# Where the turn of the heavy activations and the border's piece stand in an expert step

## The reference, cut to what matters

```python
for i in range(DEPTH):                       # DEPTH = 2, SEQ = 256, D_MODEL = 1024
    ...                                      # attention and recurrent branches
    xn2 = rmsnorm(h, ffn_norm[i])
    if i % 2 == 0:
        h = h + swiglu(xn2, dense_w1[j], dense_w3[j], dense_w2[j])
    else:
        h = h + moe_ffn(xn2, router_w[j], router_b[j], moe_w1[j], moe_w3[j], moe_w2[j])
    ...                                      # per-layer embedding

def moe_ffn(xn, router_w, router_b, w1, w3, w2):
    ...                                      # gate: top 2 of 8 experts, softmax over the two
    for e in range(N_EXPERTS):
        out = out + gate[..., e:e + 1] * swiglu(xn, w1[e], w3[e], w2[e])   # D_FF = 3584
```

## Time and profile before

| | us |
|---|---|
| median of 3 runs (1691.14 to 1693.38) | 1693.28 |
| the profiled execution, its own time | 1692.69 |
| its span, first to last instruction | 1690.8 |
| PE busy | 1671.0 |
| ACT busy, DVE busy | 877.3, 1072.1 |

### The profile page before, as it was taken

The page is one execution under the profiler, slowest core; times in us unless marked ns, Lnnn a source line. Parts: engine busy times, 40 slices in busy tenths (PEclk is TensorE's granted clock), DMA queues, the critical chain, the costliest instruction groups (busy, mean ns, idle before and its releaser), DMA issues.

```text
span 1690.8 us, 25482 instructions
## 1 busy us (share of the span) xinstructions
PE 1671.0 (99%) x10246; PEld 1299.1 (77%) x10246; DVE 1072.1 (63%) x1662; ACT 877.3 (52%) x1349; POOL 19.2 (1%) x51
## 2 busy tenths in 40 slices
PE   9999999999999999998999999999999999999998
PEld 8888999999998988996666666666656666666568
DVE  7697876665678897866644545545556455554456
ACT  6778643433356778534534445445444455454444
POOL 4000000000000000000000000000000000000000
PEclk9999999999999999998999999999999999999999
DMA  8342453633554442436999999999999999999980
GB/s 336 144 162 101 165 216 152 244 153 150 207 191 151 156 157 103 170 134 249 397 418 386 418 417 403 419 421 385 419 399 419 419 386 418 407 413 422 394 360 35
DMA packets 38124, 485.94 MB, mean 287 GB/s; under 512 B 4192, under 2 KB 6512, under 8 KB 8816
## 3 DMA queue, kind: packets, MB, share of 16 engines
q1 hardware_dynamic: 37824, 484.08, 70.8%
q10 hardware_dynamic: 176, 0.15, 0.1%
HBM read 483.15 MB, written 1.07 MB: 286 GB/s over the span
## 4 chain that ended last, share of the span: by engine, by line
PE 95%; DVE 2%; ACT 1%; DMA 0%; issue 0%; POOL 0%; DVEq 0%; ACTq 0%; POOLq 0%
PE work L1180 17%; PE work L1181 16%; PE work L1182 16%; PE acc L1528 12%; PE acc L1180 6%; PE acc L1553 6%; PE acc L1182 6%; PE acc L1181 6%; PE acc L1261 1%; PE pv_ps L1491 1%; PE misc L1447 1%; PE misc L1445 1%; PE acc L1274 1%; PE misc L1429 1%; PE acc L1299 1%; PE misc L1438 1%
## 5 line engine op out<-in xcount | busy, mean ns | idle before, releaser
L489 DVE TENSOR_TENSOR w_lo<-raw,w_hi 128x1024 fp32r<-128x1024 f32 x236 | 284.1, 1220 | 87.4 <-ACT w_hi L484 85.6
L2216 DVE TENSOR_TENSOR w_lo<-raw,w_hi 128x1024 fp32r<-128x1024 f32 x208 | 243.2, 1221 | 139.3 <-ACT w_hi L1008 139.1
L1180 PE MATMUL work<-x_r,w_hi 128*128 128x256 f32 x1024 | 297.0, 290 | 1.2 <-DVE gate_b L1978 0.6
L1181 PE MATMUL work<-x_r,w_hi 128*128 128x256 f32 x1024 | 289.5, 283 | 0.0
L1182 PE MATMUL work<-x_r,w_lo 128*128 128x256 f32 x1024 | 289.4, 283 | 0.0
L484 ACT ACTIVATE w_hi<-raw 128x1024 fp32r<-128x1024 f32 x236 | 241.8, 1048 | 66.5 <-PE acc L1182 29.1
L1008 ACT ACTIVATE w_hi<-raw 128x1024 fp32r<-128x1024 f32 x208 | 206.0, 1050 | 11.3 <-DMA raw<-in_moe_w 11.2
L1180 PEld LDWEIGHTS work<-x_r,w_hi 128*128 128x128 f32 x1024 | 196.0, 191 | 8.8 <-issue 6.2
L1181 PEld LDWEIGHTS work<-x_r,w_hi 128*128 128x128 f32 x1024 | 196.1, 192 | 1.0 <-issue 0.7
L1182 PEld LDWEIGHTS work<-x_r,w_lo 128*128 128x128 f32 x1024 | 196.1, 191 | 0.0
L1180 PE MATMUL work<-w_hi,bias_r 128*128 128x512 f32 x448 | 182.7, 408 | 2.7 <-DVE w_lo L2216 2.7
(11 more groups left out here) (356 smaller groups left out, 3128.8 us busy)
## 6 DMA issues: line engine op xcount, KB each, us to landing
raw<-in_moe_w SPq DMA_DIRECT2D x102, 2048.0 KB, 13.8
raw<-in_mix_w SPq DMA_DIRECT2D x33, 2048.0 KB, 8.1
spare<-in_moe_w SPq DMA_DIRECT2D x33, 2048.0 KB, 13.8
x<-in_moe_w SPq DMA_DIRECT2D x33, 2048.0 KB, 13.8
raw<-in_dense_w SPq DMA_DIRECT2D x21, 2048.0 KB, 8.3
raw<-in_ple_w SPq DMA_DIRECT2D x4, 2048.0 KB, 9.7
raw<-in_mix_w SPq DMA_DIRECT2D x4, 512.0 KB, 6.6
spare<-in_ple_p SPq DMA_DIRECT2D x2, 1024.0 KB, 10.3
```

Of the source, the lines that this page charges most:

```text
L489: eng.tensor_tensor(unit(w_lo, g), raw_part(g), unit(w_hi, g).bitcast(F32), ALU.subtract).then_inc(split_ok, 1)
L1180: pe.matmul(out, stat[0], move[0], start=start, stop=False, skip_group_check=True)
L1181: pe.matmul(out, stat[0], move[1], start=False, stop=False, skip_group_check=True)
L2216: dve.tensor_tensor(w_lo[u][:, :], heavy_quarter(where, i, n // HEAVY_C, n % HEAVY_C), w_hi[u][:, :].bitcast(F32), ALU.subtract).then_inc( ...
```

## The change

On PE, the turn stands behind all eight light up products in place of behind the second, and the border's piece stands directly behind the turn, ahead of the down products, in place of between the two halves of up. The turn of the light activations stands behind down 2 in place of down 1. On ACT, quarters 8 and 9 are rounded ahead of turned_hi, and the stagings out of misc stand behind the copy of the light product. On DVE, quarters 8 and 9 come between hidden and turned_lo, and add_combined behind turned_lo. No instruction is added or removed.

```diff
--- before.py
+++ after.py
@@ -1068,16 +1068,17 @@
                     if c == 0:
                         light_tokens(i)
                     if c == 4:
+                        take_gates("couple", i)
+                    for q in range(8, 10):
+                        hi_m("couple", i, n + q)
+                    turned_hi("couple", i, c)
+
+                    ge(act, l_used, "couple", i, LIGHT_N, 0, LIGHT_C * c + 3)
+                    act.activation(l_both, quad[2], ACT.Copy).then_inc(l_both_ok, 1)
+                    if c == 4:
                         stage_gathered_light(i)
-                        take_gates("couple", i)
                     if c >= 5:
                         stage_gathered(i, c - 5)
-                    turned_hi("couple", i, c)
-                    for q in range(8, 10):
-                        hi_m("couple", i, n + q)
-
-                    ge(act, l_used, "couple", i, LIGHT_N, 0, LIGHT_C * c + 3)
-                    act.activation(l_both, quad[2], ACT.Copy).then_inc(l_both_ok, 1)
                     if c == FC - 1:
                         next_tokens(i)
                     for q in range(10, 12):
@@ -1571,17 +1572,16 @@
             def couple(i):
                 for c in range(FC):
                     up("couple", i, 0, c)
-                    between(i, c)
                     up("couple", i, 1, c)
                     if c == 4:
                         turn_gates("couple", i)
                     for k in range(KT):
                         up_light(i, c, k)
-                        if k == 1:
-                            turn("couple", i, c)
+                    turn("couple", i, c)
+                    between(i, c)
                     for ft in range(FT):
                         down("couple", i, c, ft)
-                        if ft == 1:
+                        if ft == 2:
                             turn_light(i, c)
                     for ft in range(FT):
                         down_light(i, c, ft)
@@ -2231,12 +2231,12 @@
                     n = HEAVY_C * c
                     for q in range(8):
                         lo_m("couple", i, n + q)
+                    hidden("couple", i, c)
+                    for q in range(8, 10):
+                        lo_m("couple", i, n + q)
+                    turned_lo("couple", i, c)
                     if c < 4:
                         add_combined("couple", i, c)
-                    hidden("couple", i, c)
-                    turned_lo("couple", i, c)
-                    for q in range(8, 10):
-                        lo_m("couple", i, n + q)
                     if c == FC - 1:
                         next_tokens_lo(i)
                     for q in range(10, 12):
```

## The result

| | before | after |
|---|---|---|
| median, us | 1692.37 (6 runs) | 1702.98 (6 runs) |
| profiled execution, us | 1692.69 | 1701.24 |
| its span, us | 1690.8 | 1699.2 |

The ratio of after to before is 1.0064, with a 95% interval from 1.0053 to 1.0074: slower by 10.6 us. The forecast was 1700.0 us, slower by 7.4 us, with a range from 1692 to 1705; the result lies inside it.

A forecast was written before the change was run, and what follows sets the result against it. PE bounds the kernel, a step being a sum of PE pieces. Steps 0 to 3 +0.05, 4 and 5 +0.41, 6 +0.83: 1.85 a couple, four couples +7.4 on 1692.69, named 1700.0, range 1692 to 1705.

The forecast's parts named there:

- parts 1, 2, 4: PE's seams at turn and border's piece, -0.43 a step, and the wait for turned activations, +0.02 in steps 0 to 3.
- part 3: Up half 1 on PE waits for quarter 6, no longer covered by the border's piece: +0.46 in all 28 steps.
- part 5: Down 2 on PE waits for quarter 10: +0.38 in steps 4 and 5, +0.8 in step 6.
- part 1: Turn moved out of the light up products on PE: saves 0.75, gives back 0.45, net -0.30 a step.
- parts 2 and 4: Border's piece moved behind the turn, -0.13 a step; PE's wait for turned activations before down, +0.02 in steps 0 to 3.
- Part 4: Chain from turn to turned activations takes 2.08; PE waits 0.09 before down, net +0.02 in steps 0 to 3.
- B: Waits for quarters 6 and 10 cost only themselves, without exposed restarts, or DVE hands over sooner: 1695, no change; chance 0.17.
- C: Seam between half-array and full-array form alone counts; no quarter 6 wait: 1687, or 1681 with quarter 10 covered; chance 0.10.
- D: Late heavy w2 chunk delays turned_hi and PE every step; each us costs 28, 1 us gives 1728; chance 0.09.

The follow-up runs named there:

- both early on the changed kernel: Changed kernel with quarters 6 and 7 rounded ahead of silu, and splits of 10 and 11 ahead of the turned activations: 1677.96 us, 0.9920 of before.
- quarter 10 early on before: Kernel before with splits of quarters 10 and 11 moved up behind 8 and 9 on ACT and DVE: 1688.37 us, 0.9980 of before.

## Why the prediction was right, point by point

The direction, the mechanism and both places of the loss were as forecast; the size was 7.4 for 10.6 us. It was no luck of errors that cancel: the gain was put too large and the first loss too small, and both errors go the same way.

| us over the kernel | forecast | measured | from, each run less its own before |
|---|---|---|---|
| seams (parts 1, 2, 4) | -11.7 | -10.3 | both early on the changed kernel against quarter 10 early on before, (1677.96 - 1691.59) - (1688.37 - 1691.71) |
| quarter 6 (part 3) | +12.9 | +14.2 | (1702.98 - 1692.37) - (1688.01 - 1691.59) |
| quarter 10 (part 5) | +6.2 | +6.4 | (1702.98 - 1692.37) - (1692.46 - 1691.59) - (1691.71 - 1688.37) |
| sum | +7.4 | +10.3 | result +10.6 |

The interval of each of these ratios is 1.5 to 2.3 us to either side, so the differences in the table are good to some 2 or 3 us. The later turn of the light, the later stagings and the later add_combined were not run by themselves; PE shows no wait for the light activations, and the sum leaves 0.3 us for what no term holds.

**Parts 1, 2 and 4** were put at -0.43 and +0.02, so -0.41 in steps 0 to 3. The timelines say 30.35 - 29.98 = 0.37 saved. In the prediction's order part 1 was put too high: leaving the light up products saves 7.75 - 7.02, but the turn takes 0.49 in its new place and not the 0.45 that I had estimated, so 0.24 and not 0.30. The rest came close: up loses its seam of 0.20 as forecast (11.31 to 852.02 - 840.91 = 11.11), and down gives back 0.07 (0.03 in front of it, 0.04 in its restart), where parts 2 and 4 together had 0.09. Made in the other order, the moves divide otherwise: the border's piece first brings nothing, since it then stands directly behind half-array products, and the turn brings all of it, 0.37 by the timelines and 0.39 by the times (10.8 us).

**Part 3.** The wait starts and ends where it was said, 3.06 behind up half 0 (850.78 - 847.72), and a step gets longer by 30.47 - 29.98 = 0.49 when it is there; by the times it is 0.51. The 0.03 above my 0.46 lie in the triples behind the wait, which take 0.81, 0.70 and 0.69 where I had 0.80 and 0.68.

**Part 4** was right by itself: 2.07 for the forecast 2.08. The turn's 0.49 and the piece's 1.54 cover 2.03 of it, so PE stands 0.03 to 0.04 in steps 0 to 3, where 0.09 was forecast.

**Part 5** was right in its places (steps 4, 5, 6) and nearly in its size. In the first couple of the changed kernel, down loses 0.37, 0.42 and 1.67 there, for a forecast of 0.38, 0.38 and 1.58.

**The rivals.** B (waits without their restart) falls: the wait for quarter 6 takes 0.34 between two triples (1.02 - 0.68), as B would have it, but a step is 0.49 longer for it. C (faster) did not come in the changed kernel, yet it is what happens once quarter 6 is rounded ahead of silu: 3.6 us faster, where C had 5.8. D (a late chunk) did not come. But what spoke against it, that the rounding of quarter 8 never had to wait for its chunk, no longer held: it waited in 23 steps. What hides this is 4.8 us of room in the changed kernel and 0.9 with both moves, in the step shown.

By TensorEngine Tiling (Array Packing), Key Properties, of the Trainium skill a change of the tiling mode drains the engine. The trace agrees as far as it goes: with two such changes fewer (border's piece behind the turn) a step takes 0.37 less. No run separates the change of the array's form from any other stop in a run of products. One comparison speaks for the form. Before, the turn of the light stands among the fp32r products of down, with no change of form:

```profile
836.68 0.60 PE L1543 MATMUL misc<-ident,lru 128*128 128x128 f32 x4
837.04 0.48 PE L1180 MATMUL acc<-w_hi,bias_r 128*128 128x512 f32 x1
...
837.82 0.40 PE L1180 MATMUL acc<-w_hi,bias_r 128*128 128x512 f32 x1
```

Four transposes of the same size cost 837.04 - 836.68 = 0.36 and a restart of 0.10 there, 0.46 in all, against 7.75 - 7.02 = 0.73 among the half-array products.

## What to carry to other kernels

When a piece of work is moved away from between two others, ask not only what it costs in its new place but what it covered in its old one: here 1.54 us of border work, with 2.72 us of products, hid a chain of 3.06 us from the end of up half 0 over silu to the split of quarter 6, and without it PE stood 28 times. The cure was not to put the piece back but to move the evacuation that stood in front of the split on another engine's queue; that turned +10.6 us into -3.6, and with quarters 10 and 11 early too into -13.6, of which 3.3 were to be had without the change. The wait here cost more than the idle time that its row shows, so price such a wait by the distance between starts.

## What the runs showed of the hardware that was not expected

- A wait of PE that its matmul rows show as 0.18 us idle (850.78) costs 0.49 a step. Its weight load starts only when the wait is over (the PEld row at 850.78, idle for 0.60 before it), the first triple takes 0.81, and the next two run at 0.70 and 0.69 in place of 0.68.
- The same plain float32 piece costs 1.64 us directly behind half-array products and 1.54 behind the fp32r products.
- A step of 29.98 us moves its 12.6 MB at 420 GB/s, with ACT waiting up to 6.5 us for a chunk and PE never: windows with full queues (a share of 1.02 at 437 GB/s) did not mean that the transfers bound the kernel.
